# Hymba layer on one core: the order of VectorE's work over the first two weight pairs of `w_out`, and the engine that scales y

## What is computed

```python
z = rmsnorm(h, g_mix) @ w_in
x_lru, gate_lru, q, k, v = split(z)
xc = causal_conv(x_lru, conv_w, conv_b)
# RG-LRU: r, i = sigmoid gates of xc;  log_a = -8 * r * softplus(-lam)
# a = exp(log_a);  u = sqrt(-expm1(2 * log_a)) * (i * xc);  h_t = a_t * h_(t-1) + u_t
y_lru = rg_lru(xc, ...) * gelu(gate_lru)
y_attn = swa_sink_attention(q, k, v, sinks)
y = concat([rmsnorm(y_lru, g_out_lru), rmsnorm(y_attn, g_out_attn)])
h = h + y @ w_out
h = h + hier_moe(rmsnorm(h, g_moe), ...)      # 32 experts, all their weights are read
h = h + sigmoid(rmsnorm(h, g_pg) @ w_pg + b_pg) * rmsnorm(p @ w_ple, g_ple)
```

## Time and profile before

| | us |
|---|---|
| median of 3 runs (lowest, highest) | 1353.54 (1353.53, 1355.33) |
| the profiled execution's own time | 1355.54 |
| its span, first to last instruction | 1353.6 |
| PE busy / DVE busy / ACT busy / POOL busy | 1064.0 / 391.0 / 170.1 / 48.8 |
| moved from HBM | 473.12 MB read, mean 351 GB/s over the span |

### The profile page before, as it was taken

The page is one execution under the profiler, slowest core; times in us unless marked ns, Lnnn a source line. Parts: engine busy times, 40 slices in busy tenths (PEclk is TensorE's granted clock), DMA queues, the critical chain, the costliest instruction groups (busy, mean ns, idle before and its releaser), DMA issues.

```text
span 1353.6 us, 13877 instructions
## 1 busy us (share of the span) xinstructions
PE 1064.0 (79%) x5948; PEld 490.2 (36%) x5948; DVE 391.0 (29%) x528; ACT 170.1 (13%) x328; POOL 48.8 (4%) x50
## 2 busy tenths in 40 slices
PE   8999996999985786676667666766666756899998
PEld 4458884445532232222222222323232212233333
DVE  1778856863431122122112120000000000111116
ACT  1211417002210110000000000000000000010002
POOL 0111000310000011000000000000000000000000
PEclk9999998999997898888888888777787887899999
DMA  9453336356999999999999999999999999999991
GB/s 352 141 198 122 141 125 248 124 195 263 409 414 428 429 428 433 429 425 429 428 429 428 432 423 428 415 428 428 413 428 415 424 429 411 390 397 388 393 346 62
DMA packets 89468, 476.13 MB, mean 352 GB/s; under 512 B 10096, under 2 KB 10496, under 8 KB 67904
## 3 DMA queue, kind: packets, MB, share of 16 engines
q1 hardware_dynamic: 83312, 471.88, 85.6%
q0 software_dynamic: 560, 2.88, 0.6%
q10 hardware_dynamic: 5536, 0.47, 0.3%
HBM read 473.12 MB, written 2.10 MB: 351 GB/s over the span
## 4 chain that ended last, share of the span: by engine, by line
DMA 48%; PE 47%; ACT 2%; SPq 1%; DVE 1%; issue 1%; DVEq 0%
DMA ring<-in_w 47%; PE ps L1817 7%; PE ps L2005 7%; PE ps L2189 6%; PE ps L2269 4%; PE ps L2364 4%; PE ps L1790 4%; PE ps L2324 3%; PE ps L1771 2%; PE ps L2382 2%; PE ps L2155 2%; PE ps L2337 1%; PE ps L2148 1%; SPq L605 1%; SPq L524 1%
## 5 line engine op out<-in xcount | busy, mean ns | idle before, releaser
L2269 PE MATMUL ps<-ring,area 128*32 128x512 f32 x1024 | 165.1, 799 | 123.0 <-DMA ring<-in_w 123.0
L2189 PE MATMUL ps<-ring,area 128*32 128x512 f32 x976 | 146.1, 718 | 110.9 <-DMA ring<-in_w 110.9
L1547 DVE TENSOR_TENSOR h<-ps,h 128x2048 f32<-128x2048 f32 x32 | 73.3, 2291 | 286.7 <-PE ps L2155 286.6
L2269 PEld LDWEIGHTS ps<-ring,area 128*32 128x32 f32 x1024 | 43.5, 139 | 231.4 <-issue 231.4
L2189 PEld LDWEIGHTS ps<-ring,area 128*32 128x32 f32 x976 | 31.2, 121 | 207.6 <-issue 207.2
L1602 DVE TENSOR_TENSOR hT<-area,ps 128x128 f32<-128x128 f32 x16 | 4.6, 288 | 317.0 <-ACT area L1003 317.0
L2148 PE MATMUL ps<-area,hs 128*128 128x128 f32 x512 | 64.3, 279 | 0.6 <-DVE area L1528 0.6
L2324 PE MATMUL ps<-ring,hT 128*32 128x512 f32 x472 | 57.7, 620 | 7.8 <-DMA ring<-in_w 5.1
L2233 PE MATMUL ps<-ring,area 128*32 128x512 f32 x496 | 58.2, 610 | 7.0 <-DMA ring<-in_w 7.0
L2148 PEld LDWEIGHTS ps<-area,hs 128*128 128x128 f32 x512 | 59.6, 192 | 10.5 <-issue 10.5
L1817 PE MATMUL ps<-ring 128*128 128x256 f32 x256 | 56.9, 380 | 0.0
(11 more groups left out here) (334 smaller groups left out, 1102.9 us busy)
## 6 DMA issues: line engine op xcount, KB each, us to landing
ring<-in_w SPq DMA_DIRECT2D x126, 2048.0 KB, 20.7
ring<-in_w SPq DMA_DIRECT2D x63, 1024.0 KB, 15.0
ring<-in_w SPq DMA_DIRECT2D x14, 4096.0 KB, 25.1
ring<-in_w_in SPq DMA_DIRECT2D x28, 1024.0 KB, 11.1
ring<-in_w_out SPq DMA_DIRECT2D x16, 1024.0 KB, 9.7
ring<-in_w_pg SPq DMA_DIRECT2D x11, 1024.0 KB, 15.1
area<-in_w SPq DMA_DIRECT2D x2, 2048.0 KB, 14.9
hs<-in_w SPq DMA_DIRECT2D x4, 1024.0 KB, 15.0
```

The source lines that it names most:

```text
L1547: dve.tensor_tensor(h[:, t, :], ps[:, bank:bank + 4, :].rearrange("p b n -> p (b n)"), h[:, t, :], ALU.add).then_inc(acc_done, 1)
L2189: ins = mm(ps[SLOTS * g:SLOTS * g + SLOTS, 0, :], XG[:, b, k, SLOTS * e:SLOTS * e + SLOTS], s[:, D_EXP * kk:D_EXP * kk + D_EXP], start=(k ...
L2269: ins = mm(ps[SLOTS * g:SLOTS * g + SLOTS, 0, :], XG[:, b, k, SLOTS * e:SLOTS * e + SLOTS], s[:, D_EXP * kk:D_EXP * kk + D_EXP], start=(k ...
```

## The change

Four parts, with no change to what is computed nor to the number of operations on PE and DVE:

1. DVE no longer does lines 1401 and 1402 ahead of `add_product(0, 0)`, but behind the pair's fifth and sixth addition; the scans go behind the seventh addition and the first of pair 1; the product with the Gelu goes from pair 0's third addition to pair 1's second.
2. In their places stand the weight differences of pair 1, one behind each of the first three additions of pair 0. Pair 1's differences for pair 2, `ysum` and the y sums of pair 2 are put into other gaps; `y_last(2, 4)` is now the last of pair 1's work, behind `cross_difference(2)` and the mean.
3. y is scaled by the norm weights on ACT (eight `activation` with a scale per partition), directly behind the square, not on POOL.
4. PE sums the squares after pair 1's `closing`, not after its `side`, and pair 2's opening no longer waits for `msBA_ready`.

```diff
@@ gpsimd
-            pool.wait_ge(lru_act, 4)
-            for c in range(CB):
-                pool.tensor_scalar(gt[:, c, :], gt[:, c, :], prmT[:, 64 + c:65 + c], None, ALU.mult
-                                   ).then_inc(made_pool, 1)
@@ scalar
             act.activation(t1[:, :, :], gt[:, :, :], ACT.Square).then_inc(lru_act, 1)
+            act.wait_ge(lru_act, 4)
+            for c in range(CB):
+                act.activation(gt[:, c, :], gt[:, c, :], ACT.Copy, scale=prmT[:, 64 + c:65 + c]).then_inc(y_scaled, 1)
@@ vector
             step(dve.tensor_tensor(t2, t2, xc, ALU.mult))
-            dve.wait_ge(lru_act, 2)
-            step(dve.scalar_tensor_tensor(out=t1, in0=xl_flat, scalar=1.0, in1=t1, op0=ALU.add, op1=ALU.mult))
-            step(dve.tensor_tensor(t2, t2, t1, ALU.mult))
             dve.wait_ge(rBA_ready, 1)
             add_product(0, 0)
-            scan(0, 4)
+            dve.wait_ge(products_ps, PRODUCTS * (1 + LRU_GROUPS))
+            column_difference(1)
             add_product(0, 1)
-            scan(4, CB)
+            row_difference(1)
             add_product(0, 2)
-            dve.wait_ge(lru_act, 3)
-            dve.tensor_tensor(gt, gt, xc, ALU.mult).then_inc(lru_dve, 1)
+            cross_difference(1)
             add_product(0, 3)
             last_difference(0)
             add_product(0, 4)
-            dve.wait_ge(products_ps, PRODUCTS * (1 + LRU_GROUPS))
-            column_difference(1)
+            dve.wait_ge(lru_act, 2)
+            step(dve.scalar_tensor_tensor(out=t1, in0=xl_flat, scalar=1.0, in1=t1, op0=ALU.add, op1=ALU.mult))
             add_product(0, 5)
-            row_difference(1)
-            cross_difference(1)
+            step(dve.tensor_tensor(t2, t2, t1, ALU.mult))
             add_product(0, 6)
-
+            scan(0, 4)
             add_product(1, 0)
-            dve.wait_ge(lru_act, 4)
-            dve.tensor_reduce(ysum, t1.rearrange("p c t -> p t c"), AX, ALU.add).then_inc(lru_dve, 1)
+            scan(4, CB)
             add_product(1, 1)
+            dve.wait_ge(lru_act, 3)
+            dve.tensor_tensor(gt, gt, xc, ALU.mult).then_inc(lru_dve, 1)
+            add_product(1, 2)
             column_difference(2)
-            add_product(1, 2)
-            row_difference(2)
             add_product(1, 3)
             last_difference(1)
             add_product(1, 4)
-            dve.wait_ge(made_pool, CB)
+            dve.wait_ge(lru_act, 4)
+            dve.tensor_reduce(ysum, t1.rearrange("p c t -> p t c"), AX, ALU.add).then_inc(lru_dve, 1)
+            add_product(1, 5)
+            row_difference(2)
+            dve.wait_ge(y_scaled, CB)
             y_first(2, 4)
-            add_product(1, 5)
-            y_last(2, 4)
+            add_product(1, 6)
+            cross_difference(2)
             dve.wait_ge(ssA_ps, 1)
             dve.tensor_scalar(ss[:, 4:6], ps[:, ROOT_BANK, 0:NT], 1.0 / D_LRU, EPS, ALU.mult, ALU.add).then_inc(msBA_ready, 1)
-            cross_difference(2)
-            add_product(1, 6)
+            y_last(2, 4)
@@ tensor
                 if j == 2:
-                    pe_.wait_ge(msBA_ready, 2)
-                    pe_.wait_ge(made_pool, CB)
+                    pe_.wait_ge(y_scaled, CB)
                 opening(j)
                 cross(j)
                 side(j)
+                column(j)
+                tail(j)
+                closing(j, 5)
                 if j == 1:
                     pe_.wait_ge(lru_dve, 2)
...
-                column(j)
-                tail(j)
-                closing(j, 5)
```

More of the change, by code:

```diff
@@ L358, in build @@
         gates_ps, gates_ready, lru_act = sem("gates_ps"), sem("gates_ready"), sem("lru_act")
-        lru_dve, made_pool = sem("lru_dve"), sem("made_pool")
+        lru_dve, y_scaled = sem("lru_dve"), sem("y_scaled")
         lam_act, lam_sum = sem("lam_act"), sem("lam_sum")
```

## The result

| | before | changed |
|---|---|---|
| median of 6 runs, us | 1354.47 | 1344.99 |
| lowest, highest | 1353.53, 1356.09 | 1344.38, 1347.19 |
| ratio, 95% interval | | 0.9932 [0.9919, 0.9944] |
| span of the profiled execution | 1353.6 | 1343.1 |
| its own time | 1355.54 | 1345.24 |

9.5 us faster (1354.47 - 1344.99). Forecast were 1341.5 and 12.0 us: the direction and the place were right, 2.5 us of the gain are missing. The time itself is 3.5 above 1341.5, since the median of before, over six runs, is 0.9 higher than the one that I subtracted from (1353.54).

The account below looks back on a forecast made before the run. Up to 330 to 335 us PE's pace was taken to bound the kernel, then the expert weights' transfers. 14.2 gained less a 2.2 stall made 12.0 us, so median 1341.5; range 1339.0 to 1345.5.

Parts of the forecast that it names:

- The first addition ahead of the LRU's steps: Pair 0, product 3: PE no longer waits for DVE's first addition; 11.46 us plus 2.77 for the clock, together 14.2.
- The term of 2.77: Pair 0, product 3: at full clock it takes 3.44 us and not 6.21, a gain of 2.77.
- DVE keeps up in pair 0: Pair 0: DVE waits 0.7 us for a transfer, yet its additions come in time for PE; priced at nothing.
- The scaling: y's scaling on ACT: ready at 255.5, wanted at 264.8; cost between 0 and 0.7 us, taken as 0.
- My upper bound of 0.7: y's scaling: cost if ACT took POOL's 13.27 us, so y were ready at 265.5 when DVE wants it at 264.8.
- The new stall: End of pair 1: product 16 waits for y's last sum on DVE until 270.35, a loss of 2.2 us.
- The root: Start of pair 2: POOL's power after the late mean takes 2.70 us, hidden before product 17 with 0.5 to spare.
- The carry: Everything behind pair 2's opening (fourth pair, router, loads) moves along, so the 12.0 us gained reach the end.
- the sum: Whole kernel: 14.2 - 2.2 = 12.0 us gained, median 1341.5; given 0.60.
- the rival: Product 16: the new stall drops the clock, 1.7 us more lost, time 1343.2; chance 0.22.
- the clock has no reason to fall: Pair 0, product 3: without PE's idle time the clock stays up, so it takes 3.44 us and not 6.21.
- the 1.7 of the earlier trace: At 399.35, after 2.28 us without a matmul: 3.4 us at 1.2 GHz, half lost; applied to the sum it gives 10.3.

Follow-up runs that it names:

- e5: The kernel before with only y's scaling moved from POOL to ACT: 1354.75 us against 1354.84, ratio 0.9998.
- e6: The kernel before with only pair 0's first addition moved ahead of lines 1401 and 1402: 1353.47 us against 1354.84, ratio 0.9988.
- e3: The changed kernel with y's scaling put back on POOL, directly behind the square: 1344.82 us median.
- e1: The changed kernel with y's last sum and the mean moved ahead of pair 1's seventh addition and cross_difference(2): 1340.94 us median, ratio 0.9901.
- e10: e1 once more, unedited, beside the changed kernel on the same chip: 1340.66 us median, ratio 0.9901.
- e4: The changed kernel with only y_last(2, 4) moved ahead of pair 1's seventh addition, the mean left behind cross_difference(2): 1341.44 us median.
- e0: The changed kernel run again without an edit: 1345.02 us median, ratio 0.9919.
- e11: The changed kernel run a third time, unedited, beside e10: 1345.13 us median, ratio 0.9934.
- e9: The changed kernel with one more 128x2048 subtraction on DVE ahead of cross_difference(2), to lengthen PE's stall: 1346.19 us median.
- e8: The changed kernel with the mean moved ahead of cross_difference(2), y_last(2, 4) still last: 1345.64 us median.
- e7: e1 with four 128x128 matmuls filling PE's 0.78 us wait ahead of line 2079's transposes in the router: 1341.16 us median.
- e2: The changed kernel with eight 128x128 matmuls on PE between products 15 and 16, filling the stall: 1345.25 us median.

## Why the forecast was right, and where it was 2.5 us short

Between the two profiled executions 10.3 us were gained (1355.54 - 1345.24), between the medians 9.5. So of the 2.5 missing, 1.7 lie in the traces and can be found there; 0.8 lie in how each profiled execution stands to its kernel's median, 1.07 above it before and 0.25 above it now.

1. **The first addition ahead of the LRU's steps.** Right: 11.3 idle gone, first addition at 221.38, product 3 at 223.09 and 3.43 long. The term of 2.77 for product 3 at the lower clock came from one execution, 6.21; in e5, whose PE and DVE order is the old one, it is 5.43. A term smaller by 0.8 would account for the 0.8 between executions and medians. But that is argued and not shown: one other trace is no mean, and executions differ by as much elsewhere (product 1 began 1.5 sooner in e5). What is shown is that the term was a sample and not a price.
2. **DVE keeps up in pair 0.** Right: 0.73 of waiting for the transfer (0.7 forecast), product 5 not late. e6 shows that the other work in the gaps is what counts: the addition alone brings 1.4.
3. **The scaling.** Priced at nothing, and it is nothing: e5 ratio 0.9998, e3 the changed kernel's time. My upper bound of 0.7 was too high too, since POOL takes 10.05 in this order (e3) and not 13.27.
4. **The new stall.** Right in place and releaser, and near in size (1.87 idle for 2.2, product 16 at 270.20). e1, which undoes it, is 4.1 and e10 4.5 faster than the changed kernel beside them. So the stall cost twice what I had priced, 2.2.
5. **The root.** Hidden, as forecast, for the reason of a power of 1.07; with the mean late and no stall ahead of it, 0.22 shows (e4).
6. **The carry.** Right. The rest after the router is 1007.5 to 1009.4 in every kernel, whatever the front gained. The sentence under the first table that the DMA engines are not full before 350 us holds for the mean only: they are full in 215 to 230 (share 1.05) and in 305 to 320 (0.98 to 1.06), and idle again in 330 to 335. It is the idle stretch that the carry rests on.

Part 4 of the change (the sum of squares later on PE, no wait for the mean) had no run of its own. In the kernel before PE has no idle time ahead of product 15, so the wait for the mean held nothing there. With the mean now at 269.39 and product 15 at 264.65, it would have held it, so the new order needs that part; what it is worth is not measured.

**The step that failed** is a term that stood at nothing: the sum gave the stall of point 4 no cost in clock, with 0.60 for that against 0.22 for the rival. (The sentence "the clock has no reason to fall" was about product 3, and there it held.) In each of the three traces of the changed kernel some 2 us went to the clock that the sum does not have: 1.80 on product 16 (5.23 for 3.43) in the first, or, in e0 and e11, 1.9 at 317 in the router (61.35 against 59.43 before). The second kind was no rival of mine. The 1.80 accounts for the 1.7 that the traces miss. The measured time lies inside the range, but 0.5 from its upper end, and it is there because the range held the clock's rival and the spread of the runs, not because of the sum. Two of 17 times are 1340.6 and 1340.8, 0.8 below my 1341.5; that these are the executions without a fall is likely and not shown, since neither has a trace.

The Trainium skill's rule that I weighed ("TensorE: Matmul & The Clock Gate", "HAM oscillation — how this bites in real kernels": a PE that waits for its inputs starts the next burst throttled, every time), with the 1.7 of the earlier trace rows for that start, gave 10.3, nearer to the measured 9.5 than my sum. The page tells it of waits of 3 to 5 us. Here it held behind 4.20 us (e9) and, behind 1.87 to 1.91, at once in one trace of five (changed, but not e0, e3, e8, e11). Nor is a wait paid twice in proportion: e9's 2.33 more of it cost 1.1 in the median.

What stays open is where and why the clock falls in the router. The longer fall is in four of the five traces with an unfilled stall of 1.9 (e0, e3, e8, e11), and in none without one (e1, e7, e10), which speaks for a tie. But a short fall is in the same place in e4, e5 and e6, which don't have that stall. PE's instructions up to there are the same in all of them (but for e7's fill), yet the clock falls 1.6 to 2.5 us after the first logits begin in those four, 3.3 to 3.7 in e4, e5 and e6, 11.0 to 11.5 in before, changed, e7, e9 and e10, and not before the experts in e1 and e2. So what PE does in this stage does not decide it alone. That it depends on when in an execution a thin stretch comes fits all of this, but no run shows it by itself. e2 and e7 filled one wait each and did not settle it.

## What to carry to other kernels

Look at the head of the queue: an instruction that waits for a slow engine must have all work ahead of it that is needed before it, not just the next piece (1.4 us for one addition moved, 9.5 for the whole change). After such a reordering look where the queue now runs over, and put first what releases PE: one y sum moved ahead of an addition, a difference and the mean was worth 4 us more. And take a term that rests on the granted clock from several executions, since behind the same 11.30 us of idle time product 3 lost 2.8 in one and 2.0 in another.

## What the runs showed of the hardware that I had not expected

- **POOL's instructions that read SBUF stand while DVE works on two SBUF inputs.** The power of 128x2 takes 0.69 where DVE stands idle (e4), 0.70 beside an addition from PSUM (e1), 1.07 beside a sum of 0.68, 2.67 and 2.70 beside one subtraction of 2.28 (e5, before), 3.28 beside a subtraction and a sum in a row (e8). In e1 the difference begins at 267.64, when the power is nearly done, and the instruction that is caught is the next but one (2.00, where it takes 0.29 in the changed kernel). The MEMSET between them, which reads nothing, runs inside the difference and takes its usual 0.21:

```profile
267.14 0.70 POOL L670 TENSOR_TENSOR rstd<-ss,expo 128x2 f32<-128x2 f32 x1 [58.76 <-DVE ss L1434]
267.79 0.21 POOL L672 MEMSET area<- 128x128 f32 x1
268.07 2.00 POOL L673 TENSOR_SCALAR_AFFINE_SELECT area<-area 128x128 f32<-128x128 f32 x1
```

  The scalings show the same. The group of line 671 (durations in ns: least, median, most), first in the kernel before, then in e3:

```profile
L671 POOL TENSOR_SCALAR area<-area,prmT x8: 915/1527/2552, 246.0 to 258.3; 128x256 f32<-128x256 f32 x8
```

```profile
L671 POOL TENSOR_SCALAR area<-area,prmT x8: 912/918/2530, 250.7 to 259.9; 128x256 f32<-128x256 f32 x8
```

  Four of DVE's operations of 2048 elements on two inputs stand beside the eight in the kernel before, two in e3, the first of each only by its second half. Against eight times the shortest that is 5.95 more (13.27 - 7.32) and 2.75 (10.05 - 7.30): 1.4 to 1.5 for each. DVE's reduction of 3.70, which has one input, stands beside the last of e3, and from 256.6 to 260.8 five scalings are busy for 4.20: it costs them nothing. One by one, each scaling that begins inside such an operation ends 0.8 us after that operation does. The Trainium skill has a rule for it ("SBUF — State Buffer", "Who interferes with whom"): the port pair that the two share is an exclusive lock, a VectorE instruction with two SBUF inputs contends with a GpSimd instruction that reads SBUF, and who was first decides who blocks. The trace agrees for POOL. For DVE it does not show: in the kernel before a scaling runs from 248.12 to 249.04, DVE's difference begins at 248.48 in the midst of it and still takes 2.28. Of DVE's four operations there one is longer, 2.45 against 2.29 in e5, where POOL scales nothing. I had priced POOL's work by its busy time without asking what DVE does beside it.
- **The same program falls to 1.2 GHz at different places.** Product 16 behind the same 1.87 us of idle time took 5.23 in one execution of the changed kernel and 3.53 in two others (e0, e11), as in e8, where only the mean is moved. Those three lost as much 45 to 50 us later: four spans of 1343.1.
